# The entry of an attention stage in a one-core trunk kernel: head-norm spreads moved forward, narrow score products issued between the wide products of a weight unit

## The reference, cut to what matters

```python
q = rms_norm(proj[..., :NSA_Q_COLS].reshape(B, T, HKV, G, DH), q_norm)
k_cmp = rms_norm(nsa_compress(kc, ...), k_norm[0]);  v_cmp = nsa_compress(vc, ...)
s = einsum('bqhgd,bnhd->bhgqn', qb, k_cmp) * scale - slopes * dist_c      # compressed scores
p_c = masked_softmax(s, dist_c >= 0);  o_c = p_c @ v_cmp
s = einsum('bqhgd,bhqkd->bhgqk', qb, k_sel) * scale - slopes * dist_s     # and the same with k_win
p_s = masked_softmax(s, dist_s >= 0);  o_s = p_s @ v_sel
o = gb[..., 0:1] * o_c + gb[..., 1:2] * o_s + gb[..., 2:3] * o_w
```

## Time and profile before

| | |
|---|---|
| median of 3 runs | 791.24 us (789.08, 791.24, 796.52) |
| the profiled execution, its own time | 798.8 us |
| its span in the trace | 796.7 us (2.1 us lie around it) |
| TensorE busy | 765.9 us, 96% |
| mean granted TensorE clock | 0.978 of full speed |
| attention entry and items, in the trace | about 499 to 583.3 us |

### The profile page before, as it was taken

The page is one execution under the profiler, slowest core; times in us unless marked ns, Lnnn a source line. Parts: engine busy times, 40 slices in busy tenths (PEclk is TensorE's granted clock), DMA queues, the critical chain, the costliest instruction groups (busy, mean ns, idle before and its releaser), DMA issues.

```text
span 796.7 us, 18596 instructions
## 1 busy us (share of the span) xinstructions
PE 765.9 (96%) x7848; PEld 720.2 (90%) x7848; DVE 519.9 (65%) x742; ACT 380.5 (48%) x582; POOL 70.5 (9%) x52
## 2 busy tenths in 40 slices
PE   8999999998999999999999989999889999999997
PEld 6988988897879999999999979886589999999997
DVE  4896886767444887874555785667647877754441
ACT  6566543212435545444444444648746444443331
POOL 0000005370210000000000010024400000000000
PEclk9999999999989999999999999879999999999999
DMA  9853330001113599766666634200045655565541
GB/s 294 263 177 111 107 106 2 4 4 29 40 43 106 156 243 250 221 207 209 193 200 188 180 88 126 84 1 1 1 150 163 191 185 187 181 212 185 185 158 53
DMA packets 110893, 109.23 MB, mean 137 GB/s; under 512 B 7120, under 2 KB 109776, under 8 KB 110704
## 3 DMA queue, kind: packets, MB, share of 16 engines
q1 hardware_dynamic: 110832, 108.34, 45.5%
HBM read 107.28 MB, written 1.05 MB: 136 GB/s over the span
## 4 chain that ended last, share of the span: by engine, by line
PE 84%; DVE 8%; SPq 2%; ACT 2%; DMA 1%; issue 1%; POOL 1%; ACTq 0%; DVEq 0%; POOLq 0%
PE ps L450 21%; PE ps L451 20%; PE ps L452 20%; PE ps L665 4%; DMA raw<-in_rwkv_w_in 1%; DVE SB L2033 1%; DVE Gs L1691 1%; PE ps L976 1%; PE ps L762 1%; PE ps L965 1%; PE ps L813 1%; DVE nmx L2039 1%; PE ps L564 1%; PE ps L1051 1%; ACT SB L1443 1%
## 5 line engine op out<-in xcount | busy, mean ns | idle before, releaser
L1506 DVE TENSOR_TENSOR wlo<-raw,whi 128x1024 fp32r<-128x1024 f32 x188 | 225.4, 1221 | 93.1 <-ACT whi L1105 90.3
L450 PE MATMUL ps<-xh,whi 128*128 128x256 f32 x896 | 252.4, 282 | 3.7 <-issue 2.3
L451 PE MATMUL ps<-xl,whi 128*128 128x256 f32 x896 | 249.5, 278 | 0.0
L452 PE MATMUL ps<-xh,wlo 128*128 128x256 f32 x896 | 249.5, 278 | 0.0
L1105 ACT ACTIVATE whi<-raw 128x1024 fp32r<-128x1024 f32 x124 | 130.4, 1059 | 134.9 <-PE ps L452 127.1
L450 PEld LDWEIGHTS ps<-xh,whi 128*128 128x128 f32 x896 | 169.6, 189 | 7.3 <-issue 4.3
L452 PEld LDWEIGHTS ps<-xh,wlo 128*128 128x128 f32 x896 | 168.6, 188 | 0.0
L451 PEld LDWEIGHTS ps<-xl,whi 128*128 128x128 f32 x896 | 168.3, 188 | 0.3 <-issue 0.2
L452 PE MATMUL ps<-hh,wlo 128*128 128x256 f32 x512 | 142.6, 279 | 0.0
L450 PE MATMUL ps<-hh,whi 128*128 128x256 f32 x512 | 142.6, 278 | 0.0
L451 PE MATMUL ps<-hl,whi 128*128 128x256 f32 x512 | 142.6, 278 | 0.0
(11 more groups left out here) (303 smaller groups left out, 1037.5 us busy)
## 6 DMA issues: line engine op xcount, KB each, us to landing
raw<-in_mlp_w SPq DMA_DIRECT2D x128, 512.0 KB, 4.4
raw<-in_rwkv_w_in SPq DMA_DIRECT2D x24, 512.0 KB, 5.0
raw<-in_nsa_w_in SPq DMA_DIRECT2D x20, 512.0 KB, 4.4
raw<-in_rwkv_w_out SPq DMA_DIRECT2D x8, 512.0 KB, 3.5
raw<-in_nsa_w_out SPq DMA_DIRECT2D x8, 512.0 KB, 4.5
cw<-in_nsa_cmp_w SPq DMA_DIRECT2D x4, 512.0 KB, 9.9
cst<-in_consts SPq DMA_DIRECT2D x1, 1047.0 KB, 11.1
xtok<-in_x SPq DMA_DIRECT2D x2, 512.0 KB, 4.1
```

Source lines behind the costliest of these rows:

```text
L450: mm(o, wh, hi[:, kk, :], start=(kk == 0), stop=False)
L451: mm(o, wh, lo[:, kk, :], start=False, stop=False)
L452: last = mm(o, wl, hi[:, kk, :], start=False, stop=(kk == ktiles - 1))
L1506: v.tensor_tensor(wlo[:, slot, :], raw[:, slot, :], whi[:, slot, :].bitcast(f32), ALU.subtract)\
```

## The change

On TensorE all three spreads stand behind the turned roots, with `scores(1)` and `scores(2)` among them; `values(1)` follows, and takes a generator that issues one of the 16 narrow products (two matmul instructions) after the first and after the second wide matmul of each of its 8 triples, so that the last narrow product comes before the unit's last matmul. The single wait for all scaled queries becomes one wait for each pair of tiles. `transposes(0)`, `transposes(1)` and `scores(4)` move ahead of `values(2)` or between `values(2)` and `values(3)`. `weighted(0)` and `compressed_T(0)` come before `scores(5)`, not after `scores(4)`. On ACT one tiny exponential is added behind the roots, so that the exponentials' table is loaded ahead of the copy of the turned roots; the split of a later weight unit (`ahead(U0["vv"])`, a unit of the output projection) moves behind `exps(1)`, the copy of the first values (`values(0)`) from behind `exps(0)` to behind `exps(2)`, the two compressed copies each one item later. DVE's and POOL's lists are not touched.

```diff
-            def values(j):
+            def values(j, narrow=iter(())):
                         mm(o, xh[0][:, kk_, tq], wh, start=(kk_ == 0 and q == 0), ...)
+                        next(narrow, None)
                         mm(o, xh[0][:, kk_, tq], wl, start=False, ...)
+                        next(narrow, None)
                         last = mm(o, xl[0][:, kk_, tq], wh, start=False, ...)
...
-            values(1)
+            def compressed_products():
+                pe.wait_ge(sem("kcm_r"), 2)
+                pe.wait_ge(sem("vblk_r"), 4)
+                for k in range(FT):
+                    if k >= 2 and k % 2 == 0:
+                        pe.wait_ge(sem("q_scaled"), k // 2)
+                    for q in range(TT):
+                        last = mm(ps[:, 5, o:o + 32], Qn[:, k, q * P:(q + 1) * P], kcm[:, k // 2, :, :], ...)
+                        if k == FT - 1 and q == TT - 1:
+                            last.then_inc(sem("nsa_pe"), 1)
+                        yield
             spread_q(1)
+            spread_q(2)
             scores(1)
+            spread_q(3)
             scores(2)
-            spread_q(2)
-            spread_q(3)
-            pe.wait_ge(sem("kcm_r"), 2)
-            pe.wait_ge(sem("vblk_r"), 4)
-            pe.wait_ge(sem("q_scaled"), 3)
-            for q in range(TT):
-                for k in range(FT):
-                    o = q * T + k * 32
-                    last = mm(ps[:, 5, o:o + 32], Qn[:, k, q * P:(q + 1) * P], kcm[:, k // 2, :, :], ...)
-            last.then_inc(sem("nsa_pe"), 1)
+            values(1, compressed_products())
             scores(3)
+            transposes(0)
             values(2)
-            transposes(0)
+            transposes(1)
+            scores(4)
             values(3)
-            for n in range(1, len(items)):
+            pe.wait_ge(ev_act, EV0["vv"] + 1)
+            weighted(0)
+            pe.wait_ge(ev_act, EV0["vv"] + 2)
+            pe.wait_ge(sem("pc_ready"), 1)
+            compressed_T(0)
+            for n in range(2, len(items)):
...
             A(nq[:, :, :], ..., ACT.Sqrt, bias=tiny[:, 3:4]).then_inc(sem("q_root"), 1)
+            step(A(tiny[:, 2:3], tiny[:, 0:1], ACT.Exp))
             act.wait_ge(sem("nsa_pe"), NSA_PE["rq_T"])
             A(rqT[:, :], ps[0:H, 4, 0:T], ACT.Copy, scale=-1.0).then_inc(sem("rqT_ready"), 1)
-            ahead(U0["vv"])
...
-                if n == 0:
+                if n == 1:
+                    ahead(U0["vv"])
+                if n == 2:
                     values(0)
-                if n == 3:
-                    values(1)
+                if n == 4 or n == 5:
+                    compressed_copy(n - 4)
+                if n >= 2:
+                    pt_copy(n - 2)
                 if n == 2:
                     act.wait_ge(sem("csub"), 1)
                     A(Sc[:, :, :, 0:16], Sc[:, :, :, 0:16], ACT.Exp).then_inc(sem("cexp"), 1)
-                if n >= 2:
-                    pt_copy(n - 2)
-                if n == 3 or n == 4:
-                    compressed_copy(n - 3)
+                if n == 3:
+                    values(1)
```

More of the change, by code:

```diff
@@ L1038, in spread_q @@
                 last.then_inc(sem("q_spread"), 1)
+            def compressed_products():
[5 more added lines that the diff above has]
+                    for q in range(TT):
+                        o = q * T + k * 32
+                        last = mm(ps[:, 5, o:o + 32], Qn[:, k, q * P:(q + 1) * P], kcm[:, k // 2, :, :],
+                                  start=True, stop=True)
+                        if k == FT - 1 and q == TT - 1:
+                            last.then_inc(sem("nsa_pe"), 1)
+                        yield
             spread_q(1)
+            spread_q(2)
             scores(1)
+            spread_q(3)
             scores(2)
-            spread_q(2)
-            spread_q(3)
-            pe.wait_ge(sem("kcm_r"), 2)
-            pe.wait_ge(sem("vblk_r"), 4)
-            pe.wait_ge(sem("q_scaled"), 3)
-            for q in range(TT):
-                for k in range(FT):
-                    o = q * T + k * 32
-                    last = mm(ps[:, 5, o:o + 32], Qn[:, k, q * P:(q + 1) * P], kcm[:, k // 2, :, :],
-                              start=True, stop=True)
-            last.then_inc(sem("nsa_pe"), 1)
+            values(1, compressed_products())
             scores(3)
+            transposes(0)
             values(2)
-            transposes(0)
+            transposes(1)
+            scores(4)
             values(3)
-            for n in range(1, len(items)):
+            pe.wait_ge(ev_act, EV0["vv"] + 1)
[4 more added lines that the diff above has]
+            for n in range(2, len(items)):
                 if n + 3 < len(items):
@@ L1063, in _ @@
                 transposes(n)
-                if n == 1:
-                    pe.wait_ge(ev_act, EV0["vv"] + 1)
                 weighted(n - 1)
[L1067 to L1071, removed]
+                if n == 2:
+                    compressed_T(1)
             weighted(len(items) - 1)
```

## The result

| | before | after |
|---|---|---|
| median, 20 runs each | 795.28 us (789.07 to 799.17) | 801.1 us (795.54 to 810.72) |
| ratio after / before | | 1.0078, 95% interval 1.005 to 1.0106 |
| span of the profiled execution | 796.7 us | 795.9 us |

What follows compares the result with a forecast made beforehand. The attention's entry, with its narrow matmuls at 1.2 GHz, was taken to bound the end one for one: +5.3 us at the unit, -1.28 for scores(4), new waits, +4.2 at soft(6); 791.24 + 4.2 = 795.4 us, range 788.5 to 799.

Steps and rivals of the forecast that it cites:

- case A: Mixed unit: the clock stays at 1.2 GHz through the unit and into values(2); +4.2 us at soft(6); chance 0.56.
- the full load price for a narrow matmul between wide ones: Mixed unit: weight loads bound both kinds, 24 x 0.21 + 32 x 0.219 = 12.1 us at 1.2 GHz.
- the nearest row for the clock: Mixed unit: trace rows where the clock stayed low, 522.60 to 526.00, taken as grounds for 1.2 GHz to its end.
- B: Mixed unit: the clock comes back inside it; -0.4 to +1.3 us at soft(6), middle +0.5; chance 0.26.
- C: Mixed unit: the clock is already high at its start, unit 6.4 us; -1.6 to -5.4 us at soft(6); chance 0.10.
- D: Mixed unit: narrow matmuls hide between wide ones, 5.0 to 8 us; -3.0 to +0.2, middle -1.4; chance 0.04.
- E: Steady part: the ring of DVE, ACT and TensorE absorbs the shift, so 0 at the end; chance 0.04.
- the step from soft(4) to soft(6): Behind the unit: from 538.3 over exps(4), the compressed copy and weighted(1) to soft(6) at 544.6.
- at most 1 us of DVE's idle time: Behind the unit: cost of compressed_T(0), ahead of scores(5), waiting for the gates and ACT's copy of the values.
- weighted(1)'s L1003 waits for L1433: Sign in the trace after, before soft(6): weighted(1) waits for the compressed copy, which ends at 542.3.
- some +1.5 us: Behind the unit: if the clock stays low longer, values(2) and (3) become late for ACT's copy.
- the base: Whole kernel: the median before, 791.24 us, to which the shift was added unscaled; a median of few off by 1.5 to 2.

Runs made afterwards that it cites:

- after_narrow_run: Changed kernel, but the second unit of values is issued without the narrow products, whose 32 instructions follow it in one run; ratio to the kernel before 1.0014.
- after_fill24: Changed kernel with 24 more wide matmuls, whose results nobody uses, just before the mixed unit; ratio to the kernel before 1.0035.
- before_mixed2: Kernel before, but narrow products issued between the wide matmuls of the third unit of values, moved in front of scores(3); no spread moved; ratio to before 1.0033.
- after_again: The changed kernel's same text run once more, for a second clock record; ratio to the kernel before 1.0066.
- after_waits_moved: Changed kernel with scores(5) ahead of compressed_T(0) and the first compressed copy directly behind the window values' copy, the second behind pt_copy(2); ratio to before 1.0072.
- clock_kept: Against the kernel before: all values units cut into pieces between sums, spreads and scores, square sums and narrow products mixed with wide matmuls; ratio 1.0026.
- wide_first: Against the kernel before: values(2) as a run before the narrow run, spreads through banks 4 and 5, scores(4), scores(5) and compressed copies moved; ratio 0.9968.

## Why the prediction was right and wrong

**The direction and the mechanism were right.** The steps up to DVE's read of the narrow products came out within 0.2 us, after 1.2 us are taken off the positions after: spreads at 507.9 (forecast 508.0), 0.46 us each for the first eight and 0.50 for the last four (0.46), start of the unit at 516.8 (516.7), its length 11.95 us (12.1), DVE's read at 528.8 (528.8), soft(4) at 538.4 (538.3). The clock stayed at 1.2 GHz through the unit and into values(2), as in case A. after_narrow_run, after_fill24 and before_mixed2 show that this is the cause and not only a companion of the loss.

**The two choices that decided** hold: the full load price for a narrow matmul between wide ones (11.95 us low, 6.46 high, against 12.1 and 6.4), and the nearest row for the clock (522.60 to 526.00 in the earlier trace rows, where scores and a few wide matmuls did not bring it back). The row was near, not certain: in after_again scores and transposes did. Cases B, C and D are refuted in both records of the kernel after, and so is E: the shift is still 4.1 us at the output projection, and the time shows it.

**What failed.** The forecast was 795.4 us and the median 801.1, 5.7 us more. Of these 1.6 us lie in the shift (5.8 between the medians, against 4.2) and 4.0 us in the base.

**What failed in the sum is a term**, the step from soft(4) to soft(6), taken as 6.3 us. The prediction let it hang on exps(4) and the compressed copy, 544.6, and put the wait of compressed_T(0) at "at most 1 us of DVE's idle time". It measured 545.6, and the step 7.2 us (6.7 in after_again). compressed_T(0) waited for the copy of the last values, because values(2) and (3) stand behind the unit and begin there with the clock low, and scores(5), transposes(2), weighted(1) and scores(6) run in TensorE's one queue behind it. The sign "weighted(1)'s L1003 waits for L1433" did not come: in after these products follow without a gap, and the wait appears in after_narrow_run, where the clock is high behind the unit and the step, 6.4 us, is close to the forecast. The text had named this, "some +1.5 us", but only for a longer low clock; it was due in the likeliest case already. The shift at soft(6) is +5.2 us, not +4.2. after_waits_moved shows that moving the copy does not heal it.

**The larger part of the miss is the base.** The sum was put on the median of the three runs shown, 791.24 us; over 20 runs the kernel before takes 795.28, 4.0 us more. The prediction had allowed 1.5 to 2 us for it. With 791.24 the measured shift of 6.2 us would have ended at 797.4, inside the range; the medians ended at 801.1, outside. The forecast shift of +4.2 us itself lies at the lower edge of the measured interval, 4.0 to 8.4. The profiled execution of before, 798.8 us, is 3.5 us above the median of many, about as far as the median of three lies below it.

**What stays open:** the timed loss, 6.2 us, is larger than the 4.1 us by which the output projection starts later in the traces of both records (91.5 against 87.4). From soft(6) to that point the record of before takes 45.0 us, with 6.8 us of low clock at the last items, and that of after 43.9, with 3.4; so the records flatter the change there by 1.1 us. Behind it they differ the other way by 6.1 us, though a low stretch (592.03 to 595.44) stands only in the record of after. That is the beat of the wide matmuls, told above. How often either kernel takes the slower beat, and whether the order of the entry has a part in it, no record shows; it may hold the rest of the loss.

## What to carry to other kernels

Put no mix of wide and narrow matmuls where TensorE's clock is already low and other engines wait for it: a run of the wide ones first and the narrow ones behind it cost 8.15 us here, the same instructions mixed 11.95. Before wide work is taken away from a stretch of small matmuls and given to a later one, read from the clock column what ended the low stretches of the trace; and follow every instruction that stands behind a moved wait on the same queue, since here the values, not the gates, were late. Split two profiled spans by stage before you compare them: here 6.1 us of difference lay in a part that no edit touched. A shift of 5 us in a kernel whose executions scatter by 10 is to be put on a base of many runs, or told as a shift alone.

## What the runs showed that was not expected

The same 56 matmuls, mixed, kept a high clock for 6.46 us in after_fill24 and left a low clock low for 11.95 us in the kernel after and for 12.01 us in before_mixed2: what the mix does depends on the clock that it finds. In clock_kept it ran 23.9 us at 2.4 GHz with spreads, scores and pieces of values among one another. Stretches of scores and spreads behave either way: in the kernel before the clock fell behind them at 515.76, in wide_first, with the same order up to there, it did not. And when the square sums were mixed into wide matmuls the fall only moved from the end of the sums' run to the scores behind them (514.16), and cost what it had cost. A low clock ended behind scores and transposes, with 0.03 us of wide matmuls, in after_again. And at the same granted clock, 1.00, wide matmuls followed one another every 0.117 us in some records and every 0.113 in others.
